# A fused encoder step on one core: twelve slots for raw expert weights in place of six, and who makes the first low parts

## What is computed

```
def hmoe(h, w_rg, b_rg, w_re, b_re, w_gate, w_up, w_down):
    """Two-level routing: top-1 group, then top-2 experts inside it; exact sparse dispatch."""
    g_logits = (hf @ w_rg + b_rg)
    g_sel = jnp.argmax(g_logits, axis=-1)
    ...
    top_v, top_i = lax.top_k(e_logits, TOP_K)
    wts = jax.nn.softmax(top_v, axis=-1) * p_g
    ...
    def expert_block(args):
        xi, e = args
        return (jax.nn.silu(xi @ w_gate[e]) * (xi @ w_up[e])) @ w_down[e]
```

## Time and profile before

| | |
|---|---|
| median of three runs | 1139.31 us (1138.9 to 1141.3) |
| the profiled execution | 1138.3 us, its span 1136.5 us |
| TensorE products busy | 1025.3 us (90%), weight loads 931.5 us (82%) |
| VectorE, ScalarE, GpSimd busy | 623.3 us (55%), 523.4 us (46%), 82.7 us (7%) |
| chain that ended last | TensorE 72%, DMA 10%, VectorE 9%, ScalarE 5% |
| read from HBM | 174.40 MB |

### The profile page before, as it was taken

One profiled execution on the slowest core, in us unless ns is written; L12 is line 12 of the kernel. 1 busy time (PEld: TensorE's weight loads), 2 busy tenths in 40 slices (PEclk: granted clock), 3 DMA queues, 4 the chain that ended last, 5 costly groups with the idle time before them and its releaser, 6 DMA issues.

```text
span 1136.5 us, 17499 instructions
## 1 busy us (share of the span) xinstructions
PE 1025.3 (90%) x7238; PEld 931.5 (82%) x7238; DVE 623.3 (55%) x892; ACT 523.4 (46%) x694; POOL 82.7 (7%) x98
## 2 busy tenths in 40 slices
PE   3999999999999999999999899961899999999950
PEld 2999999899999889889988799961688888787840
DVE  5122943333125664565342563257498988988836
ACT  6125723232223454544343421151478787777832
POOL 3300000000000000000100100032001010010003
PEclk9999999999999999999999999975899999999975
DMA  8673462547456252214853522074599999999836
GB/s 193 191 96 57 60 93 54 62 91 101 99 102 152 41 72 41 72 38 105 192 149 113 189 75 75 1 273 166 195 343 399 399 399 399 398 399 396 339 114 236
DMA packets 110762, 198.02 MB, mean 174 GB/s; under 512 B 10448, under 2 KB 55504, under 8 KB 110688
## 3 DMA queue, kind: packets, MB, share of 16 engines
q1 hardware_dynamic: 99888, 157.76, 49.9%
q0 software_dynamic: 7872, 28.58, 6.7%
q10 hardware_dynamic: 2928, 10.62, 2.4%
HBM read 174.40 MB, written 22.54 MB: 173 GB/s over the span
## 4 chain that ended last, share of the span: by engine, by line
PE 72%; DMA 10%; DVE 9%; ACT 5%; issue 3%; ACTq 0%; POOL 0%; DVEq 0%; POOLq 0%
PE ps L940 21%; PE ps L942 20%; PE ps L941 20%; DMA raw<-in_w_up_dram 7%; PE ps L925 4%; DVE e_lo L1627 2%; ACT e_hi L828 2%; PE ps L1112 2%; PE ps L1096 1%; DVE x L1690 1%; PE ps L1066 1%; PE ps L1044 1%; DMA ring<-in_w_in_dram 1%; ACT w_hi L638 1%; PE ps L1081 1%
## 5 line engine op out<-in xcount | busy, mean ns | idle before, releaser
L1627 DVE TENSOR_TENSOR e_lo<-raw,e_hi 128x2048 fp32r<-128x2048 f32 x94 | 214.7, 2289 | 51.0 <-ACT e_hi L828 50.5
L828 ACT ACTIVATE e_hi<-raw 128x2048 fp32r<-128x2048 f32 x96 | 184.1, 1917 | 74.6 <-PE ps L942 40.5
L940 PE MATMUL ps<-h_hi,w_hi 128*128 128x272 f32 x640 | 190.3, 297 | 5.0 <-DVE h_lo L1294 3.9
L942 PE MATMUL ps<-h_hi,w_lo 128*128 128x272 f32 x640 | 186.0, 291 | 0.0
L941 PE MATMUL ps<-h_lo,w_hi 128*128 128x272 f32 x640 | 185.2, 289 | 0.0
L1301 DVE TENSOR_TENSOR w_lo<-ring,w_hi 128x2048 fp32r<-128x2048 f32 x42 | 96.2, 2291 | 96.8 <-ACT w_hi L638 96.8
L940 PE MATMUL ps<-w_hi,h_hi 128*128 128x256 f32 x480 | 136.6, 285 | 0.0
L941 PE MATMUL ps<-w_lo,h_hi 128*128 128x256 f32 x480 | 135.6, 283 | 0.0
L942 PE MATMUL ps<-w_hi,h_lo 128*128 128x256 f32 x480 | 134.6, 280 | 0.0
L940 PEld LDWEIGHTS ps<-h_hi,w_hi 128*128 128x128 f32 x640 | 121.7, 190 | 12.7 <-issue 7.9
L941 PEld LDWEIGHTS ps<-h_lo,w_hi 128*128 128x128 f32 x640 | 121.8, 190 | 0.2
(11 more groups left out here) (350 smaller groups left out, 1914.8 us busy)
## 6 DMA issues: line engine op xcount, KB each, us to landing
ring<-in_w_in_dram SPq DMA_DIRECT2D x32, 1024.0 KB, 9.4
raw<-in_w_gate_dram SPq DMA_DIRECT2D x32, 1024.0 KB, 12.1
raw<-in_w_up_dram SPq DMA_DIRECT2D x32, 1024.0 KB, 12.7
raw<-in_w_down_dram SPq DMA_DIRECT2D x32, 1024.0 KB, 11.7
y_rows<-yo ACTq DMA_DIRECT2D x16, 512.0 KB, 6.2
y_rows<-att POOLq DMA_DIRECT2D x8, 512.0 KB, 7.7
ring<-in_w_proj_a_dram SPq DMA_DIRECT2D x4, 1024.0 KB, 5.4
kraw<-in_cache_k_dram SPq DMA_DIRECT2D x4, 1024.0 KB, 9.3
```

Of the source, the lines that this page charges most:

```text
L828: act.activation(e_hi[:, buf], raw[:, slot], ACT.Copy).then_inc(s_ehi, 1)
L940: pe.matmul(out, left[0], right[0], start=first, stop=False)
L942: return pe.matmul(out, left[1], right[0], start=False, stop=final)
L1627: dve.tensor_tensor(e_lo[:, buf], raw[:, slot], e_hi[:, buf].bitcast(F32), ALU.subtract).then_inc(s_elo, 1)
```

## The change

Twelve raw slots take the place of six: nine from the start of the ring on (`raw9`), two where the low part of the gated sum was (`raw2`), one behind the sample gate's place (`raw1`). A table `PHYS` gives each of the six parts of an even and of an odd expert its slot. The low part is written over the raw part (`lo9`, `lo2`, `lo1` name the same bytes), the three buffers of `e_lo` go, and SP refills a slot when TensorE is done with the part in it (`used`, by `s_part`) and no longer when its low part is made. Five parts (four of expert 0, one of expert 1) are loaded from SP's queue ahead of the load of the last projection tile, into slots that the last projection doesn't use.

GpSimd makes no low parts. ScalarE makes the first three high parts before the routing's exponentials; VectorE makes the first three low parts right after `slot_i`, and the table of overflows (`overflow`) after the first tokens are taken apart. To make room, the gathered tokens `xg`, the hidden rows `hh` and the output `yo` have one buffer in place of two, so the gather for an expert waits for the transposes of the one before. `XT(1)` moves behind the third block of the first expert.

```
+        PHYS = ((5, 6, 7, 8, 3, 4), (11, 0, 1, 2, 9, 10))
+        raw9, lo9 = at(W, "raw9", [P, 9, PART]), at(W, "lo9", [P, 9, PART], F32R)
...
@@ sync
+                elif n == len(wtiles) - 2:
+                    emptied(sp, units_of["pb"][-1])
+                    for j in range(4):
+                        load_part(0, j, 0)
+                    load_part(1, 0, 1)
+            def used(r, j, odd):
+                sp.wait_ge(s_part, part_of(r, j, odd)[0] + 1)
             sp.wait_ge(s_unit, last_unit + 1)
...
-            for j in range(PARTS):
-                load_part(0, j)
...
-            with sp.Fori(2, NE) as r:
-                for j in range(PARTS):
-                    before = part_of(r - 1, j)[0]
-                    sp.wait_ge(s_elo, before + 1)
-                    load_part(r if j < 4 else r - 1, j)
+            for j in range(1, 4):
+                load_part(1, j, 1)
+            for side in range(2):
+                for j in (4, 5):
+                    load_part(side, j, side)
+            for j in range(4):
+                used(0, j, 0)
+                load_part(2, j, 0)
...
+            with sp.Fori(2, NE // 2) as it:
+                for odd in range(2):
+                    for j in range(PARTS):
+                        used(it * 2 + (odd - 2), j, odd)
+                        load_part(it * 2 + (odd if j < 4 else odd - 1), j, odd if j < 4 else 1 - odd)
             for j in (4, 5):
-                sp.wait_ge(s_elo, part_of(NE - 1, j)[0] + 1)
-                load_part(NE - 1, j)
+                used(NE - 2, j, 0)
+                load_part(NE - 1, j, 1)
@@ gpsimd
-            for j in range(2):
-                seq, buf, slot, _ = part_of(0, j)
-                pool.wait_ge(s_ehi, seq + 1)
-                pool.tensor_tensor(e_lo[:, buf], raw[:, slot], e_hi[:, buf].bitcast(F32), ALU.subtract).then_inc(s_elo, 1)
             pool.wait_ge(s_slot, 1)
...
             for e in range(NE):
-                if e >= 2:
-                    pool.wait_ge(s_xt, e - 1)
-                gather(e, e % 2)
+                if e:
+                    pool.wait_ge(s_xt, e)
+                gather(e)
@@ scalar
-            part_hi(part_of(0, 0))
+            act.wait_ge(s_unit, last_unit + 1)
+            for j in range(PBUF):
+                part_hi(part_of(0, j, 0))
             act.wait_ge(s_gd, 1)
...
@@ vector
-                    dve.tensor_tensor(e_lo[:, buf], raw[:, slot], e_hi[:, buf].bitcast(F32), ALU.subtract).then_inc(s_elo, 1)
+                    dve.tensor_tensor(lo_of(slot), raw_of(slot), e_hi[:, buf].bitcast(F32), ALU.subtract).then_inc(s_elo, 1)
...
-            dve.wait_ge(s_elo, 2)
-            part_lo(part_of(0, 2))
+            for j in range(PBUF):
+                part_lo(part_of(0, j, 0))
             x_out(0, 0)
-            part_lo(third_after(0, 0))
+            overflow()
+            part_lo(third_after(0, 0, 0))
+            part_lo(third_after(0, 1, 0))
             x_out(1, 1)
```

More of the change, by code:

```diff
@@ L276, in build @@
         s_slot, s_ovi = sem("s_slot"), sem("s_ovi")
-        s_raw = [sem(f"s_raw{i}") for i in range(PARTS)]
+        s_raw = [s_x[i] if i < NTILE else sem(f"s_raw{i}") for i in range(2 * PARTS)]
         s_ehi, s_elo = sem("s_ehi"), sem("s_elo")
         s_part = sem("s_part")
-        s_xg = [sem("s_xg0"), sem("s_xg1")]
+        s_xg = sem("s_xg")
         s_xt, s_xhi, s_xlo = sem("s_xt"), sem("s_xhi"), sem("s_xlo")
@@ L427, in vals, with load_part @@
                 sp.dma_start(vc[:], src).then_inc(s_vc, 16)
+            def load_part(e, j, side):
+                w, n = ((w_gate, FE), (w_up, FE), (w_down, D))[j // 2]
+                c = PART // n
+                src = w[0, bass.ds(e, 1)].rearrange("a (c p) n -> p (a c) n", p=P)[:, c * (j % 2):c * (j % 2) + c]
+                slot = PHYS[side][j]
+                sp.dma_start(raw_of(slot).rearrange("p (c n) -> p c n", c=c), src).then_inc(s_raw[slot], 16)
             with nc.allow_non_contiguous_dma("a few parameter columns"):
@@ L607, in _ @@
                     pool.wait_ge(s_xt, NE + i)
-                    gather(NE + i, 0)
-            pool.wait_ge(s_yst[0], 16 * NE // 2)
-            pool.wait_ge(s_yst[1], 16 * NE // 2)
+                    gather(NE + i)
+            pool.wait_ge(s_yst, 16 * NE)
             pool.wait_ge(s_exdone, 1)
@@ L1180, in _, with XT @@
             last.then_inc(s_tok, 1)
-            def XT(e, slot, count):
-                pe.wait_ge(s_xg[slot], count)
-                transposes(P, [(ps[:, 4 + c // 4, P * (c % 4):P * (c % 4) + P], xg[:, slot, P * c:P * c + P]) for c in range(KC)], s_xt)
+            def XT(e):
+                pe.wait_ge(s_xg, e * 16 + 16)
+                transposes(P, [(ps[:, 4 + c // 4, P * (c % 4):P * (c % 4) + P], xg[:, P * c:P * c + P]) for c in range(KC)], s_xt)
             def GU(part, slot):
-                seq, buf, j, _ = part
+                seq, buf, j, place, _ = part
+                lo = lo_of(place)
                 pe.wait_ge(s_elo, seq + 1)
@@ L1192, in GU, with AT @@
                     c, w = KC // 2 * (j % 2) + i, slice(FE * i, FE * i + FE)
-                    last = three_products(ps[:, j // 2], (x_hi[:, slot, c], x_lo[:, slot, c]), (e_hi[:, buf, w], e_lo[:, buf, w]),
+                    last = three_products(ps[:, j // 2], (x_hi[:, slot, c], x_lo[:, slot, c]), (e_hi[:, buf, w], lo[:, w]),
                                           c == 0, c == KC - 1)
                 last.then_inc(s_part, 1)
-            def AT(e, slot):
+            def AT(e):
                 pe.wait_ge(s_hh, e + 1)
-                transposes(P, [(ps[:, 2, P * c:P * c + P], hh[:, slot, P * c:P * c + P]) for c in range(FE // P)], s_at)
+                transposes(P, [(ps[:, 2, P * c:P * c + P], hh[:, P * c:P * c + P]) for c in range(FE // P)], s_at)
             def Dn(part):
-                seq, buf, j, _ = part
+                seq, buf, j, place, _ = part
+                lo = lo_of(place)
                 pe.wait_ge(s_elo, seq + 1)
```

226 lines of the change are left out of this document (113 added, 113 removed).

## The result

| | before | after |
|---|---|---|
| median of the runs of this comparison | 1140.3 us (1138.9 to 1142.48) | 1126.13 us (1125.12 to 1126.58) |
| profiled execution, its span | 1138.3, 1136.5 us | 1125.12, 1123.4 us |

The ratio is 0.9875, with a 95% interval of 0.986 to 0.9891: 14.2 us faster. The forecast was 1123.5 us with a range of 1119.5 to 1128.5; the time lies in it, 2.6 us above the forecast.

What follows compares the result with a forecast made beforehand. The prediction blamed two stretched VectorE routing operations and, late in the experts, the DMA. Terms -7.9 + 1.7 - 3.7 - 3.6 - 1.7 = -15.2 gave 1123.1 (profiled) or 1124.1 us (median); it said 1123.5, range 1119.5 to 1128.5.

Steps and rivals of the forecast that it cites:

- The routing: Routing before the experts: without GpSimd's two low parts, two VectorE operations of about 4 us shrink to normal length, -7.9 us.
- The first gather: Gather behind slot_i: held by VectorE's first low part, it takes 2.8 us in place of 1.15, +1.7 us.
- A: Rival: the first gather is not held up by VectorE's low part; 1121.8 us, chance 0.10.
- B: Rival: the first gather waits for all three low parts, +6.2 in place of +1.7; 1128 us, chance 0.10.
- Early loads: Five parts loaded during the last projection: nothing lost and little gained, put at 0.
- The lead of twelve slots: Expert loop: the deeper lead of loads lets TensorE keep its pace though the DMA falls behind 0.6 us per expert.
- C: Rival: the DMA loses its 399 GB/s with many loads in flight; at 359 GB/s 1126 us, chance 0.06.
- D: Rival: with a single token buffer TensorE waits for the gather at 14 experts; up to 1167 us, chance 0.03.
- The pace: Third to last expert's token transposes: 17.77 us per expert throughout, 234.68 us becomes 231.0, -3.7 us.
- The first blocks: First gate product to the third expert's token transposes: no change, 0; the clock's rise only a 2 us uncertainty.
- The end: Last token transposes to last hidden transposes: 32.3 us falls to 28.7, -3.6 us.
- The last downs: Last two blocks: 7.2 us becomes 5.5 at full clock, -1.7 us, with bounds 0 to 1.7.

Runs made afterwards that it cites:

- e1: Changed kernel with the first two low parts given back to GpSimd, one left to VectorE; 1132.66 us, 0.9953 of the kernel before.
- e2: Changed kernel with the overflow table back between slot_i and the low parts, one low part behind the first tokens' low part; 1124.66 us.
- e3: Kernel before, six slots kept; only the first low parts move from GpSimd to VectorE and the overflow table behind the first tokens; 1134.63 us.
- e6: Changed kernel with slots refilled later than possible, last two loads excepted: by eight blocks 1214.15 us, by four blocks 1124.83 us.
- e4: Changed kernel with hh_lo placed right behind hh_hi and hh put where hh_lo was; 1125.46 us, 0.9889 of the kernel before.
- e10: Changed kernel with hh_lo right ahead of hh_hi, which keeps its place, and hh where hh_lo was; 1125.6 us.
- e9: Changed kernel with overflow table ahead of low parts, hh_lo beside hh_hi, and 21, 9, 22 and 9 unread products in TensorE's waits; 1117.13 us.
- e7: Changed kernel with unread products added: 32 ahead of the first token transposes, 40 behind the first expert's fourth block; 1127.97 us.

## Why the prediction was right, and where it was not

**The routing** (-7.9) measured -7.84, and e1 brings it back by giving GpSimd its work: shown.

**The first gather** (+1.7) measured +1.78. The mechanism is shown by e2, e1 and the later gathers; the pieces differ a little. The gather starts 0.57 us later than I assumed, but its end hangs on the low part, so it is 2.23 us long in place of 2.8 and ends where the forecast had it. Why it starts later is open. A and B both fall.

**Early loads** (nothing, "little is gained") failed as a step: they are worth 2.0 us, because they are through before the gather. In the sum it did no harm, since I had put the gather's landing at its undisturbed time, and the early loads are what keeps it so.

**The lead of twelve slots**: the loads left the chain, as said; the DMA kept 396 to 401 GB/s, so C falls. The 358 GB/s of the Trainium skill (SBUF — State Buffer, Summary: rules for kernel authors) was not what this core got. e3 shows that the slots and not the move of the low parts do this; e6 that seven blocks' lead in the loop suffice and three do not. A single token buffer (D) costs nothing: GpSimd's next gather starts right behind the transposes, and behind 788.41 TensorE waits only twice more for over 0.3 us, 5.30 us for the first hidden rows and 2.53 us ahead of the last down products, never for tokens.

**The pace** (-3.7) is the term that was mis-sized: -2.40. I had taken the 17.77 us of the undisturbed experts before as a constant of TensorE, although the change moves operands in SBUF. hh_lo's new place puts the down products 0.005 us farther apart, 0.13 us per expert or 1.7 us in 13; e4 and e10 give 1.8 us back. That is more than the 1.3 that were missing, because the gate and up products took 0.04 us per expert less than before, which the prediction did not have either and which no run explains. The prediction named a pace other than 17.8 with nothing waiting as what would overturn its sum most; it was that, in small.

**The first blocks** (0) were +1.72 in the first profile and +0.62 in the second. The trace shows a half clock of 5.5 us behind the first product where it was 3.4 before, and of 6.0 us behind the wait for the hidden rows where it was 5.3; half of the difference is lost, 1.4 us. The other 0.3 is that wait itself, 5.30 us where it was 4.99. The windows of these two places, the granted clock third from the right, first of the kernel before:

```profile
795.70:807.70 12.00, 12.00 (x50) 9.92 (x51) 4.44 (x3) 5.70 (x4) 1.28 (x1) 0.86 0.31 99
...
814.30:820.00 5.70, 5.66 (x17) 4.40 (x17) 0.00 (x0) 0.12 (x1) 0.00 (x0) 0.53 0.89 313
```

and of the changed kernel:

```profile
788.40:794.00 5.60, 5.58 (x13) 4.43 (x14) 1.65 (x7) 0.00 (x0) 0.00 (x0) 0.51 0.20 80
...
808.30:814.40 6.10, 6.01 (x17) 4.74 (x17) 0.04 (x1) 0.42 (x1) 0.00 (x0) 0.50 0.08 32
```

In the second profile of the same program the two stretches at half clock are 6.2 and 3.0 us long. The prediction had this only as an uncertainty of 2 us; e9 shows that idle time is the cause, by filling it. Why the half clock lasts up to 3 us longer in one execution than in the next is open.

**The end** (-3.6) measured -3.61. **The last downs** (-1.7) were -1.37 in the first profile but +0.17 in the second: after 2.53 us of idle time the clock falls in some executions and not in others (5.8 us in four and 7.1 to 7.4 in seven of the eleven profiles of the changed kernel and its variants that have this wait). The bounds of 0 to 1.7 held; the middle would have been the better choice.

**The sum.** In the profiled execution the pace is 1.3 us above the forecast, the first blocks 1.7, the last downs 0.3 and three small stretches 0.3 together; that makes 3.6. It is 2.1 us above in all, because 1.2 us up to lg and 0.3 behind the last downs came off; both stretches differ by more than that between kernels with the same instructions there. So the mechanism of each large term is borne out, but that the time lies as near as it does to the forecast is in part luck.

## What to carry to other kernels

A load that is "hidden anyway" should be set against every transfer that it shares the DMA with, not only against the work that needs it: here the early loads pay through a gather that they don't feed. When a change moves buffers, don't carry a product's spacing over as a constant; compare it in both traces, per operand. Where TensorE waits a few microseconds at a known place, products whose results nobody reads can hold its clock, but what runs over the wait is lost: 32 and 40 of them ran over by 1.6 and some 2 us and brought no gain, while 21, 9, 22 and 9 brought 6.8 us in the stretches behind them, with 0.9 lost where the 21 ran over.

## What the runs showed of the hardware

- A stationary operand's place in SBUF changed the distance of fp32r products from 0.227 to about 0.232 us with the same instructions and the same clock; moving it by 32 bytes to a multiple of 64 took back one of the three distances in a triple of products, and laying it beside the other half all three.
- An indirect DMA's issue on GpSimd that began inside a VectorE subtraction with both inputs in SBUF ended 0.8 to 0.9 us behind it (2.23 and 2.83 us long for the first gather; 0.81 us behind it for 13 later gathers of the changed kernel). It took 1.02 us beside small operations, and 0.94 us inside a subtraction with one input in PSUM.
- Beside GpSimd's subtractions of 4.5 us, VectorE operations of some 0.2 us took 3.83 to 4.36 us, one of them a TENSOR_SCALAR with a single tensor input; a TENSOR_REDUCE and two additions from PSUM kept their 0.15 to 0.24 us.
- In e7 the granted clock fell to its lower level, 1.2 GHz, about 1 us into the products behind a wait of 2.37 us, although TensorE had been kept busy for 8.7 us and eight transposes ahead of that wait. Behind waits of about 2.5 us ahead of the last down products the products ran at half clock for a time in seven profiles and not in four.
